# Level-0 part of a triangular inverse: VectorE 32x32 block transposes in place of TensorE transposes

## What is computed

```python
lower = jnp.tril(jnp.einsum('...id,...jd->...ij', kb, kc) * decay, -1)
a_mat = lower + jnp.eye(c, dtype=f32)
rhs = jnp.concatenate([vc * bc[..., None], kb * jnp.exp(gcum)[..., None]], axis=-1)
sol = lax.linalg.triangular_solve(a_mat, rhs, left_side=True, lower=True, unit_diagonal=True)
```

## Time and profile before

| | us |
|---|---|
| median of 3 runs | 2078.92 (2078.46 to 2079.14) |
| the profiled execution | 2080.27 |
| its span in the profile | 2078.4 |
| PE busy | 2007.6 (97%) |
| PE weight load busy | 1943.6 (94%) |
| DVE busy | 1197.8 (58%) |
| ACT busy | 734.8 (35%) |
| POOL busy | 677.5 (33%) |

### The profile page before, as it was taken

How to read it: one execution, slowest core, us unless ns; L and a number is a source line. 1 busy time by engine, 2 the same in 40 slices (tenths; PEclk the granted TensorE clock), 3 DMA queues, 4 the chain that set the end, 5 groups by cost and what they waited for, 6 DMA issues and landing times.

```text
span 2078.4 us, 38361 instructions
## 1 busy us (share of the span) xinstructions
PE 2007.6 (97%) x16255; PEld 1943.6 (94%) x16255; DVE 1197.8 (58%) x2198; ACT 734.8 (35%) x1236; POOL 677.5 (33%) x642
## 2 busy tenths in 40 slices
PE   4999999999999999999899989999999999999996
PEld 4999999999999989889899989999999999989996
DVE  6545555555553335664533359999998954463333
ACT  5322322222222213553322235555555543342220
POOL 3023123222311222000311138888888840021110
PEclk9999999999999999999999999999999999999998
DMA  5311111111121234212343423333332322223332
GB/s 169 107 42 63 63 62 53 63 63 58 57 69 62 93 141 143 76 58 67 105 128 128 134 69 91 94 93 93 97 96 81 87 93 71 82 80 123 104 105 97
DMA packets 74956, 185.11 MB, mean 89 GB/s; under 512 B 26360, under 2 KB 26680, under 8 KB 74536
## 3 DMA queue, kind: packets, MB, share of 16 engines
q1 hardware_dynamic: 66672, 163.59, 25.2%
q0 software_dynamic: 3504, 9.63, 1.4%
q10 hardware_dynamic: 4608, 9.44, 1.2%
HBM read 163.56 MB, written 19.06 MB: 88 GB/s over the span
## 4 chain that ended last, share of the span: by engine, by line
PE 43%; DVE 4%; POOL 3%; issue 1%; ACT 0%; POOLq 0%; DVEq 0%; ACTq 0%
PE acc L535 43%; POOL arena L2039 2%; DVE full L1411 1%; DVE act_lo L1408 1%; DVE gp L1411 1%; DVE w_lo L1408 0%; PE gp L592 0%; PE gp L577 0%; DVE full L1408 0%; DVE arena L1408 0%; POOL out_cfs L2277 0%; DVE arena L1411 0%; ACT arena L1270 0%; POOLq L202 0%; POOL small L2039 0%
## 5 line engine op out<-in xcount | busy, mean ns | idle before, releaser
L535 PE MATMUL acc<-act_hi,w_hi 128*128 128x288 f32 x4128 | 914.4, 303 | 2.5 <-DVE w_lo L1408 1.8
L535 PE MATMUL acc<-act_hi,w_lo 128*128 128x288 f32 x4128 | 884.0, 296 | 0.0
L535 PE MATMUL acc<-act_lo,w_hi 128*128 128x288 f32 x4128 | 883.1, 296 | 0.0
L535 PEld LDWEIGHTS acc<-act_hi,w_hi 128*128 128x128 f32 x4128 | 660.1, 189 | 24.2 <-issue 14.7
L535 PEld LDWEIGHTS acc<-act_hi,w_lo 128*128 128x128 f32 x4128 | 664.6, 189 | 0.0
L535 PEld LDWEIGHTS acc<-act_lo,w_hi 128*128 128x128 f32 x4128 | 664.4, 189 | 0.0
L2039 POOL TENSOR_TENSOR arena<-arena 128x512 f32<-128x512 f32 (+1 forms) x266 | 374.9, 1409 | 353.2 <-ACT arena L1270 308.1
L985 ACT ACTIVATE w_hi<-w_raw 128x1024 fp32r<-128x1024 f32 x266 | 279.7, 1054 | 441.3 <-PE acc L535 291.0
L1408 DVE TENSOR_TENSOR w_lo<-w_raw,w_hi 128x1024 fp32r<-128x1024 f32 x266 | 383.8, 1462 | 39.6 <-ACT w_hi L985 38.8
L1411 DVE SCALAR_TENSOR_TENSOR gp<-arena,par,gp 128x64 f32<-128x64 f32 (+1 forms) x688 | 248.0, 441 | 0.0
L985 ACT ACTIVATE arena<-arena,par 128x512 f32<-128x512 f32 x240 | 165.3, 720 | 104.8 <-POOL arena L2039 93.3
(11 more groups left out here) (253 smaller groups left out, 1517.3 us busy)
## 6 DMA issues: line engine op xcount, KB each, us to landing
w_raw<-wt SPq DMA_DIRECT2D x266, 512.0 KB, 3.9
full<-x SPq DMA_DIRECT2D x8, 576.0 KB, 8.9
arena<-x SPq DMA_DIRECT2D x16, 288.0 KB, 3.6
x_scratch<-full ACTq DMA_DIRECT2D x16, 288.0 KB, 4.0
arena<-x_scratch SPq DMA_DIRECT2D x16, 288.0 KB, 2.8
out_y<-full ACTq DMA_DIRECT2D x16, 288.0 KB, 2.4
arena<-state_in SPq DMA_DIRECT2D x6, 512.0 KB, 4.4
out_sdn<-arena POOLq DMA_DIRECT2D x6, 512.0 KB, 3.1
```

The lines of the kernel that those rows point to most:

```text
L535: ins = pe.matmul(acc[:, s, i, 0:HALF], w[:, s, wk], a[:, k, i * HALF:(i + 1) * HALF], start=(k == 0 and j == 0), stop=(k == KT - 1 and j ...
```

## The change

TensorE's step `m0` is gone, for heads and sampled tokens. DVE makes `Xt` first, straight from `mtl[0]` as before, and then `X` as the 32x32 block transposes of `xt`: two `dve.transpose` of 64x256 for a head, one of 64x512 for the sampled tokens. `a1` waits for `X`, now the later one. `L2` no longer waits for `m0`. In the first head the two memsets stand between `Xt` and the transposes.

```diff
-DVE_PLAN = {1: ["kg"], 2: ["dmask"], 3: ["ssum"], 4: ["vs", "Mt", "attn"], 6: ["X", "Xt"]}
+DVE_PLAN = {1: ["kg"], 2: ["dmask"], 3: ["ssum"], 4: ["vs", "Mt", "attn"], 6: ["Xt", "X"]}
...
-                elif name == "m0":
-                    pe.wait_ge(pool_h.sem, pool_h.at("L0", it))
-                    pe.wait_ge(dve_h.sem, dve_h.at("vs", it))
-                    for c in range(NC):
-                        ins = pe.transpose(gp[:, 0, ck(c)], mtl[0][:, c, :], ident)
                 elif name[0] == "a":
                     l = int(name[1])
                     pe.wait_ge(pool_h.sem, pool_h.at(f"L{l}", it))
-                    pe.wait_ge(dve_h.sem, dve_h.at("Xt" if l == 1 else f"X{l - 1}", it))
+                    pe.wait_ge(dve_h.sem, dve_h.at("X" if l == 1 else f"X{l - 1}", it))
...
-                elif name == "m0":
-                    pe.wait_ge(samp_pool, SP_["L0"])
-                    for h in range(H):
-                        ins = pe.transpose(gp[0:NS, 2, sc(h)], mtl_s[0][:, h, :], ident[0:NS, 0:NS])
...
+                elif name == "Xt":
+                    dve.wait_ge(pool_h.sem, pool_h.at("L0", it))
+                    ins = tt(xt, per_group(ident, NC), mtl[0], SUB)
                 elif name == "X":
-                    pe_at("m0")
                     if isinstance(it, int) and it == 0:
                         for h_, other in (diagonal, diagonal[::-1]):
                             dve.memset(a1[h_, :, other], 0.0)
+                    dve.wait_ge(dve_h.sem, dve_h.at("Xt", it))
                     for h_ in diagonal:
-                        ins = tt(x_d[h_], per_group(ident[h_, h_], NC), bank4(0)[h_, :, h_], SUB)
-                elif name == "Xt":
-                    ins = tt(xt, per_group(ident, NC), mtl[0], SUB)
+                        ins = dve.transpose(x_d[h_], xt[h_, :, h_])
...
+                elif name == "Xt":
+                    dve.wait_ge(samp_pool, SP_["L0"])
+                    ins = tt(xt_s, ids, mtl_s[0], SUB)
                 elif name == "X":
-                    pe_at("m0")
-                    ins = tt(x_s, ids, b64(gp[0:NS, 2, :]), SUB)
-                elif name == "Xt":
-                    ins = tt(xt_s, ids, mtl_s[0], SUB)
+                    own("Xt")
+                    ins = dve.transpose(x_s, xt_s)
...
-                    if l >= 2:
-                        pool.wait_ge(pe_h.sem, pe_h.at("m0" if l == 2 else f"a{l - 2}", it))
+                    if l > 2:
+                        pool.wait_ge(pe_h.sem, pe_h.at(f"a{l - 2}", it))
```

More of the change, by code:

```diff
@@ L97 @@
 LV = range(1, LEVELS)
-PE_HEAD = (["kv_tok", "gcum", "norm", "gram", "m0"] + [f"{s}{i}" for i in LV for s in ("a", "x")]
+PE_HEAD = (["kv_tok", "gcum", "norm", "gram"] + [f"{s}{i}" for i in LV for s in ("a", "x")]
            + ["u0", "so0"] + [f"{s}{c}" for c in range(1, NC) for s in ("s", "u", "so")] + ["o_chan"])
@@ L101 @@
 assert LEVELS == 7
-DVE_HEAD = (["kg", "dmask", "ssum", "vs", "Mt", "attn", "X", "Xt"]
+DVE_HEAD = (["kg", "dmask", "ssum", "vs", "Mt", "attn", "Xt", "X"]
             + [n for i in LV for n in [f"X{i}"] + [f"T{i}"] * (i in IN_BLOCKS)]
@@ L108 @@
              + ["f1", "f2", "f3", "f4", "f5"])
-PE_PLAN = {1: "kv_tok", 2: "gcum", 3: "norm", 4: "gram", 6: "m0"}
-PE_PLAN |= {7 + i: n for i, n in enumerate(PE_HEAD[5:-1])}
+PE_PLAN = {1: "kv_tok", 2: "gcum", 3: "norm", 4: "gram"}
+PE_PLAN |= {7 + i: n for i, n in enumerate(PE_HEAD[4:-1])}
 def counts(names):
     return {n: i + 1 for i, n in enumerate(names)}
-_groups = [["k_tok"], ["v_tok"], ["norm"], [], ["gram"], ["gcum"], [], [], ["m0"], ["a1"], ["x1"], ["a2"], ["x2"]]
+_groups = [["k_tok"], ["v_tok"], ["norm"], [], ["gram"], ["gcum"], [], [], [], ["a1"], ["x1"], ["a2"], ["x2"]]
 SAMP_PLAN = [[(n, None) for n in g] for g in _groups] + [[] for _ in range(13, 48)]
@@ L128 @@
 SPE = counts([n if h is None else f"{n}{h}" for g in SAMP_PLAN for n, h in g])
-SD = counts(["kg", "ssum", "vs", "dmask", "dmask2", "Mt", "Mtb", "attn", "X", "Xt", "X1", "Xt1", "Xt2"]
+SD = counts(["kg", "ssum", "vs", "dmask", "dmask2", "Mt", "Mtb", "attn", "Xt", "X", "X1", "Xt1", "Xt2"]
             + [f"{s}{h}" for g in range(H // 2) for s, h in (("r", g), ("vp", g), ("o", g), ("S", 2 * g), ("S", 2 * g + 1))]
@@ L148 @@
 _at = {(n if h is None else f"{n}{h}"): i for i, g in enumerate(SAMP_PLAN) for n, h in g}
+_at["low"] = _at["a1"] - 1
 _after = {"kg": "k_tok", "ssum": "norm", "vs": "v_tok", "dmask": "gcum", "dmask2": "gcum", "Mt": "gcum",
-          "Mtb": "gcum", "attn": "gcum", "X": "m0", "Xt": "m0", "X1": "x1", "Xt1": "x1", "Xt2": "x2",
+          "Mtb": "gcum", "attn": "gcum", "X": "low", "Xt": "low", "X1": "x1", "Xt1": "x1", "Xt2": "x2",
           "on": f"ns{H - 1}"}
@@ L766, in samp_step @@
                     pe.wait_ge(samp_pool, SP_[f"L{l}"])
-                    pe.wait_ge(samp_dve, SD["Xt"] if l == 1 else SD["Xt1"])
+                    pe.wait_ge(samp_dve, SD["X"] if l == 1 else SD["Xt1"])
                     for h in range(H):
```

## The result

| | before | changed |
|---|---|---|
| median of the comparison's runs | 2082.38 (2078.34 to 2094.31) | 2095.49 (2086.68 to 2100.16) |
| ratio | | 1.0045 (95%: 1.0025 to 1.0066) |
| profiled execution | 2080.27, span 2078.4 | 2088.79, span 2087.0 |

What follows compares the result with a forecast made beforehand. TensorE, busy 97%, was taken to bound the kernel, but VectorE's chain sets the pace at `a1`. Heads +7.4 and sampled tokens +0.3 gave +7.7 us: 2088.0 from the profiled execution, 2086.6 by the median; range 2083.5 to 2089.5.

Steps and rivals of the forecast that it cites:

- What bounds the place: At `a1`, VectorE's chain sets the pace, not TensorE; `m0`'s removal brings TensorE there 0.46 us earlier, worth nothing.
- TensorE's busy time: A sign in the changed profile: PE's busy time should fall by some 4 us while the span grows.
- `Xt` queues behind `L1`: In each head `Xt` waits for POOL's `L1` on the shared port, lasts about 1.7 us, ends 0.56 behind `L1`.
- `Xt` goes first: Rival at the port: `Xt` goes ahead of `L1`; +0.15 a head, 2080.4 us, no change; 6%.
- the two engines run side by side: Rival at the port: `Xt` and `L1` overlap; -0.14 a head, 2077.0 us, no change; 3%.
- The transposes: Behind `Xt` on VectorE: 0.90 us for a head's pair, 0.70 for the sampled tokens' 64x512 one.
- The later `a1`: In each head `a1` starts 0.93 us later than before; eight heads give +7.4 us (6.2 to 8.6).
- the sampled tokens: Once, `a1` at 706.41 in place of 706.15: +0.3 us (bounds -0.8 to +0.5).
- The sum of these terms: Whole kernel: +7.4 us for the heads and +0.3 for the sampled tokens give +7.7 us.
- the term for the wait of head 0: Head 0's `a1` at 123.93 in place of 123.00, also 0.93 later; a wait of about 1.65 in every head.
- the term for the level and spread of the runs: Whole time: profiled execution 1.35 above the runs' median; one more us on both sides for runs and small shifts.
- The rival on the clock: TensorE's clock falls in the longer waits at `a1`, each head losing 3.5 us: +28, 2114 us; 2%.

Runs made afterwards that it cites:

- m0 kept: The changed kernel with the four transposes of `m0` put back on TensorE in the heads, read by nobody; one run, 2080.68 us.
- Both: The changed kernel with `Xt` and `X` in front of `w_lo`, and `L1` waiting for `Xt`; median 2083.34 us, ratio 0.9991 (0.9971 to 1.0010).

## Why the prediction was right and where it was wrong

*What bounds the place* held: `a1` waits for VectorE's chain, and TensorE's saved work is worth nothing (m0 kept: same stretch but for the dip). TensorE's busy time fell by 1.6 us, not by some 4; that was not taken apart.

*`Xt` queues behind `L1`* held in size: 1.77 against "about 1.7", 0.68 with `L1` out of the way, 1.76 when Xt was moved and `L1` not. The rivals that `Xt` goes first, or that the two engines run side by side, fell with it.

*The transposes* take 0.89 against 0.90, and the 64x512 one 0.70, as taken. The later `a1` measured 0.92 a head against 0.93, the sampled tokens +0.28 against +0.3. The sum of these terms, +7.7, stands.

Two steps failed: the term for the wait of head 0, and the term for the level and spread of the runs, which is the larger one. The measured median is 2095.49 - 2086.6 = 8.9 above the forecast. 3.5 of it is the level of the kernel before, 1.5 is head 0's, and the other 3.9 lie within the spread of the runs and belong to no step that a trace shows.

*Head 0.* The text worked out a start of `a1` 0.93 later there too, and left the wait at 1.65, "in every head". But head 0 waited 0.90 before, not 0.26, so that its wait had to become 0.90 + 0.46 + 0.93, near 2.3. Behind that wait TensorE's clock fell. The rival on the clock was there, with 2% and for all heads alike, and looked at a row with a wait of 1.7 that kept its clock; it wasn't asked whether any of the eight waits would be longer. It cost +1.5.

*The level and the range.* The forecast started from the median of three runs within 0.7 us, and allowed one us for the runs. Over 35 runs the kernel before lies between 2077.74 and 2093.12, and its median in the three sets of runs was 2082.38, 2084.53 and 2088.96, not 2078.92. Over the 35 runs the time rises by some 1.4 us for each 0.001 that the mean granted clock is lower (0.982 to 0.991, correlation -0.84). In the traces the spread goes with dips of 3.4 us to half clock, none to about nine of them from 680 to 820 us (0, 6 in the kernel before; 1, 7 in the changed one). By the ratio, 2078.92 x 1.0045 = 2088.3 would have been within the range. The difference of 9.4 agrees with 7.7 + 1.5, but its interval is too wide to show the 1.5: that is shown by the head stretch alone. That the dips between 680 and 820 are as frequent in both kernels is not shown: there are too few traces of each.

## What to carry to other kernels

Before moving an operation, look at what runs beside it on the other engine: here a VectorE step that read PSUM filled just the time in which POOL held the port, and the step that took its place, with both inputs in SBUF, could not. Taking work from the busiest engine pays only where that engine isn't waiting; where it waits, shorten the chain first (here by order alone), and then the same edit wins. And where a change lengthens waits, list each one's new length, not a typical one: here the clock fell behind the longest of eight and behind no other. And before giving a range in microseconds, look at the spread of more than three runs.

## What the runs showed that was not expected

The dense transposes of the sampled tokens hold POOL up, unlike those of the heads. In the changed kernel:

```profile
716.09 0.70 DVE L1704 STREAM_TRANSPOSE arena<-arena 64x512 f32<-64x512 f32 x1
716.72 1.18 DVE L1400 TENSOR_TENSOR w_lo<-w_raw,w_hi 128x1024 fp32r<-128x1024 f32 x1
716.20 2.84 POOL L2033 TENSOR_TENSOR arena<-arena,cst 64x512 f32<-64x512 f32 x1 [0.69 <-DVE arena L1400]
```

`L2` is issued at 716.20 beside the transpose alone, yet lasts 2.84, and `w_lo`, issued half a microsecond behind it, is not held up (1.18). `L2` ends 1.14 behind `w_lo`, about its own length. So by these times it began only behind `w_lo`: the transpose kept it out, and `w_lo` went ahead of a POOL product that had been waiting, against the order seen everywhere else. In two parts of 64x256 it is the same (0.76 for both, `L2` 2.90). In a head `L2` beside a pair of transposes (197.64, 1.27) is not slowed. Nor is it the `w_lo` right behind: with Xt and X in front of w_lo it stands there in the heads too, and yet `L2` takes its 1.27 (195.18) and `w_lo` waits for it (1.54 in place of 1.21). In the heads one side of the transpose is strided, here both are dense. That is the one difference in form that I see besides the tensors and the partitions; the cause was not tried. It is also why `a1` of the sampled tokens waited 2.3 us for `L1` where `L1` had to wait for `Xt`: there `L1` met the transpose and `w_lo` in the same way (issued at 708.21, and `L1` and `L2` together 4.05).

At head 0's `a1` single waits of 1.6 and 1.8 us left TensorE's clock at 2.4 GHz, and waits of 2.2 (three traces of three) took it to 1.2 for about 3.4 us, at a price of 1.5 us. The length of the wait alone doesn't decide it, though. `a1` of the sampled tokens waited 2.26 where `L1` waits for Xt, and the clock stayed full:

```profile
711.09 1.14 PE L761 MATMUL gp<-arena 64*64 64x64 f32 x16 [2.26 <-POOL arena L2033]
...
700.00:720.00 20.00, 17.74 (x171) 1.00 0.07 24
```

It did so behind the 2.13 of "Both" as well. And all twelve traces have a wait of 3.0 for ACT between 999 and 1024 us. Behind it the clock fell in eight of them and stayed full in four. Here are the first trace of the kernel before and the second, in this order:

```profile
1000.00:1020.00 20.00, 17.18 (x124) 1.00 0.36 109
...
1000.00:1020.00 20.00, 15.57 (x102) 0.91 0.09 30
```

In the sampled tokens' stretch dips of the same kind come without a wait in front of each and in different numbers from run to run (none to about nine); in "Both" one began at 719.6 us behind six microseconds in which TensorE was busy throughout. What sets them off is open, and so is why head 0's wait of 2.2 met one each time.
